# A mixer and mixture-of-experts kernel: weight loads held back behind two row gathers, VectorE work reordered around them, fewer filler products

## The reference, cut to what matters

```python
logits = jnp.dot(t.astype(jnp.float32), router_w.astype(jnp.float32))
probs = jax.nn.softmax(logits, axis=-1)
...
g_idx = jnp.argmax(group_score, axis=-1)            # one of 4 groups of 4 experts
_, loc = lax.top_k(in_group, TOP_K)                 # two experts of the group
combine = ...                                       # weights of the two, in a row of 16
g = jnp.einsum('td,edf->tef', t, w_gate)            # d = 1024, f = 512, e = 16
u = jnp.einsum('td,edf->tef', t, w_up)
a = jax.nn.silu(g) * u * combine[:, :, None]
y = jnp.einsum('tef,efd->td', a, w_down)
return rmsnorm(x + g_f * y, final_norm_g)
```

## Time and profile before

| | |
|---|---|
| median of 3 runs | 761.75 us |
| the runs | 761.73, 763.98, 761.75 us |
| the profiled execution, its own time | 763.88 us |
| its span | 761.5 us |
| TensorE busy | 738.6 us (97%) |
| VectorE busy | 584.9 us (77%) |
| ScalarE busy | 392.0 us (51%) |
| GpSimd busy | 149.2 us (20%) |
| mean granted TensorE clock | 0.995 of full |
| chain of waits, by engine | PE 82%, DVE 9%, DMA 4%, issue 2% |

### The profile page before, as it was taken

The page is one execution under the profiler, slowest core; times in us unless marked ns, Lnnn a source line. Parts: engine busy times, 40 slices in busy tenths (PEclk is TensorE's granted clock), DMA queues, the critical chain, the costliest instruction groups (busy, mean ns, idle before and its releaser), DMA issues.

```text
span 761.5 us, 10492 instructions
## 1 busy us (share of the span) xinstructions
PE 738.6 (97%) x3447; PEld 606.9 (80%) x3447; DVE 584.9 (77%) x709; ACT 392.0 (51%) x360; POOL 149.2 (20%) x121
## 2 busy tenths in 40 slices
PE   7999999999999999999999899999999999999995
PEld 6888888776888888887789677888888888888884
DVE  5884326764675766748768889999999999999985
ACT  5536333424222141323435267777777777777744
POOL 1000004102000000000054272523322323222313
PEclk9999999999999999999999999999999999999999
DMA  8989414211375472927372728799999999999992
GB/s 304 337 290 372 141 56 145 75 57 57 110 248 169 161 250 88 337 72 275 139 246 113 282 73 308 287 398 410 358 358 395 366 375 386 378 396 390 343 182 110
DMA packets 108996, 187.30 MB, mean 246 GB/s; under 512 B 7367, under 2 KB 58631, under 8 KB 108972
## 3 DMA queue, kind: packets, MB, share of 16 engines
q1 hardware_dynamic: 101420, 173.63, 62.9%
q0 software_dynamic: 5936, 11.71, 5.5%
q10 hardware_dynamic: 1616, 1.65, 0.7%
HBM read 180.00 MB, written 15.79 MB: 257 GB/s over the span
## 4 chain that ended last, share of the span: by engine, by line
PE 82%; DVE 9%; DMA 4%; issue 2%; ACT 1%; SPq 1%; POOL 0%; DVEq 0%; POOLq 0%; ACTq 0%
PE ps L1581 25%; PE ps L1583 25%; PE ps L1582 24%; DVE wsplit L893 2%; PE ps L1839 2%; PE ps L1931 1%; PE ps L1711 1%; DMA raw<-in_w_ada 1%; DVE raw L982 1%; DMA raw<-in_w_in 1%; PE ps L1772 1%; DMA raw<-in_w_out 1%; DVE raw L936 1%; PE ps L1875 1%; DMA work<-hf_rows,tok_idx 1%
## 5 line engine op out<-in xcount | busy, mean ns | idle before, releaser
L893 DVE TENSOR_TENSOR wsplit<-raw,wsplit 128x2048 fp32r<-128x2048 f32 x128 | 291.0, 2287 | 67.7 <-ACT wsplit L615 34.6
L802 ACT ACTIVATE wsplit<-raw 128x2048 fp32r<-128x2048 f32 x96 | 183.6, 1919 | 62.4 <-PE ps L1583 62.4
L1581 PE MATMUL ps<-wsplit,hgT 128*128 128x512 f32 x264 | 104.4, 395 | 1.1 <-DVE hgT L1363 1.1
L1583 PE MATMUL ps<-wsplit,hgT 128*128 128x512 f32 x264 | 103.0, 390 | 0.0
L1582 PE MATMUL ps<-wsplit,hgT 128*128 128x512 f32 x264 | 102.8, 389 | 0.0
L1581 PE MATMUL ps<-hT,wsplit 128*128 128x512 f32 x256 | 101.1, 395 | 1.1 <-DVE mx L1078 1.0
L1582 PE MATMUL ps<-hT,wsplit 128*128 128x512 f32 x256 | 99.6, 389 | 0.0
L1583 PE MATMUL ps<-hT,wsplit 128*128 128x512 f32 x256 | 99.6, 389 | 0.0
L936 DVE SCALAR_TENSOR_TENSOR raw<-raw,c_silu 128x256 f32 (+1 forms) x128 | 62.0, 485 | 13.7 <-DMA raw<-in_w_ada 9.7
L1581 PEld LDWEIGHTS ps<-wsplit,hgT 128*128 128x128 f32 x264 | 49.6, 188 | 11.1 <-issue 1.3
L1583 PEld LDWEIGHTS ps<-wsplit,hgT 128*128 128x128 f32 x264 | 49.5, 188 | 10.7
(11 more groups left out here) (310 smaller groups left out, 1214.0 us busy)
## 6 DMA issues: line engine op xcount, KB each, us to landing
raw<-in_w_exp_gate SPq DMA_DIRECT2D x32, 1024.0 KB
raw<-in_w_exp_up SPq DMA_DIRECT2D x32, 1024.0 KB
raw<-in_w_exp_down SPq DMA_DIRECT2D x32, 1024.0 KB
raw<-in_w_in SPq DMA_DIRECT2D x20, 1024.0 KB
raw<-in_w_ada SPq DMA_DIRECT2D x16, 1024.0 KB
raw<-in_w_ada SPq DMA_DIRECT2D x16, 512.0 KB, 5.6
expert_rows<-tmp SPq DMA_DIRECT2D x4, 1024.0 KB, 9.7
raw<-in_w_branch_a SPq DMA_DIRECT2D x4, 1024.0 KB
```

Of the source, the lines that this page charges most:

```text
L802: A_(wsplit[:, c, 0, :], raw[:, c, :], ACT.Copy).then_inc(hi_ready, 1)
L893: V.tensor_tensor(wsplit[:, n, 1, :], raw[:, slot, :], wsplit[:, n, 0, :].bitcast(F32), ALU.subtract).then_inc(lo_ready, 1)
L1581: nc.tensor.matmul(out, w_hi, m_hi_, start=first, stop=False)
L1583: return nc.tensor.matmul(out, w_lo, m_hi_, start=False, stop=last)
```

## The change

Three places change. SP now issues only the first half of `w_down[0]` ahead of a wait for gather 0; the second half follows that, and the two halves of `w_up[1]` wait for gather 1 as well. VectorE does `indices(1)` and tile 0's low rows ahead of the second up chunk's low part and of the two table steps, and `rows_lo(1)` ahead of `select(2, ...)` and of slot 1's low part, where it stood behind both. TensorE issues 7 filler products, not 16, ahead of its wait for gather 0.

```diff
             sp.wait_ge(hf_saved, 16 * NT)
             load(0, w_gate[1, :, 0:4, :], 4)
-            for c in range(2):
-                load(c + 4, w_down[0, :, 2 * c:2 * c + 2, :], 2)
+            load(4, w_down[0, :, 0:2, :], 2)
+            sp.wait_ge(gathered, 16)
+            load(5, w_down[0, :, 2:4, :], 2)
+            sp.wait_ge(gathered, 32)
             for c in range(2):
                 sp.wait_ge(lo_ready, M0 + 3 + c)
                 load(c + 2, w_up[1, :, 4 * c:4 * c + 4, :], 4)
...
             V.tensor_copy(slot_of[:, :], r_slots).then_inc(slots_ready, 1)
             ie = [P, TILES_MAX, E]
-            lo_n(M0 + 3, 3)
-            step(V.tensor_tensor(r_le, iota1[:, 0:TILES_MAX].unsqueeze(2).broadcast_to(ie),
-                                 r_cum.unsqueeze(1).broadcast_to(ie), ALU.is_gt))
-            done()
-            step(V.tensor_reduce(r_n, r_le, AX_X, ALU.add))
-            done()
-
             indices(1)
             for half in range(2):
                 dve.wait_ge((first_hi_half, hg_hi)[half], 1)
...
+            lo_n(M0 + 3, 3)
+            step(V.tensor_tensor(r_le, iota1[:, 0:TILES_MAX].unsqueeze(2).broadcast_to(ie),
+                                 r_cum.unsqueeze(1).broadcast_to(ie), ALU.is_gt))
+            done()
+            step(V.tensor_reduce(r_n, r_le, AX_X, ALU.add))
+            done()
...
             dve.wait_ge(hi_ready, M0 + 5)
             lo(0, 0)
+            rows_lo(1)
             select(2, expert_ahead(0))
...
                 lo_c(1)
                 if not prev:
-                    rows_lo(i + 1)
                     indices(i + 2)
                 lo_c(2)
...
             index(1)
-            unread_products(16)
+            unread_products(7)
             pe.wait_ge(gathered, 16)
```

More of the change, by code:

```diff
@@ L1405, in _ @@
             ie = [P, TILES_MAX, E]
+            indices(1)
+            for half in range(2):
+                dve.wait_ge((first_hi_half, hg_hi)[half], 1)
+                h_half = first_hi[:, 4 * half:4 * half + 4, :].rearrange("p k m -> p (k m)").bitcast(F32)
+                V.tensor_tensor(first_lo[:, 4 * half:4 * half + 4, :].rearrange("p k m -> p (k m)"),
+                                ps[:, 2 + half, :], h_half, ALU.subtract).then_inc((first_lo_half, hg_lo)[half], 1)
             lo_n(M0 + 3, 3)
@@ L1411, in _ @@
             done()
[L1413 to L1418, removed]
             step(V.tensor_tensor(r_le, r_le, r_cum.unsqueeze(1).broadcast_to(ie), ALU.mult))
```

## The result

The changed kernel is slower. Its median is 766.87 us (7 runs, 765.19 to 768.72) against 762.5 us of the kernel before (7 runs beside it, 761.63 to 763.98). The ratio is 1.0056, with a 95% interval of 1.0041 to 1.0071. The forecast was 763.3 us with a range up to 765.7 and no measurable difference; the time lies above the range.

The account below looks back on a forecast made before the run. TensorE, busy for 97% of the span, was taken to bound the kernel, its wait for VectorE at tile 2's gate counting. Gather 0 (0), gather 1 (0) and VectorE's order (+1.5) on 761.75 gave 763.3 us, range 761.2 to 765.7.

Parts of the forecast that it names:

- What bounds the seam: Between 420 and 470 us, the chain runs through POOL's table rows to gather 1, not gather 0, whose gain is swallowed.
- Gather 1 does not follow: POOL's third table-row DMA meets the moved low part, so gather 1 still starts near 440.4: 0 us (-0.3 to +0.9).
- The other moved loads cost nothing: `w_down[0]`'s second half has 20 us until VectorE wants it, and gather 2 is wanted over 10 us on.
- VectorE's order: Behind gather 1, `select(2)` and a low part move behind `rows_lo(1)`; tile 2's gate starts at 472.8, 1.5 us later.
- +1.5: The forecast's sum in us: 0 for gather 0, 0 for gather 1, all of it for VectorE's order.
- The clock rival: Clock falls in the 4.0 us wait for gather 1: +2.4 to +3.3 in all, 764.2 to 765.1 us; chance 0.22.
- The fast rivals: Gather 1 sooner: POOL slips past the low part (762.1 us, 0.12), or free queues shorten its DMAs (759.9 us, 0.08).
- The runs' levels: A median drawn from the runs' upper level, 2.2 us higher (765.5), whatever the change does; chance 0.08.

Follow-up runs that it names:

- first profile: The changed kernel with no further edit, its first profiled execution: 768.72 us, seam 40.36 us from `slot_of` to tile 2's first gate product.
- third profile: The changed kernel run a third time with no further edit: 767.72 us (one run), seam 43.86 us.
- filled variant: The changed kernel with 14 filler products in TensorE's wait for gather 1, ahead of tile 1's turn: median 767.15 us, ratio 1.0056, seam 40.60 us.

## Why the prediction was wrong, point by point

The seam can be split at the start of tile 1's transposes. The last column says what the chain of waits runs through in the second part.

| | `slot_of` to tile 1's transposes | from there to tile 2's gate | bound by |
|---|---|---|---|
| before | 11.96 | 26.28 | TensorE |
| `rows_lo(1)` moved, alone | 11.94 | 27.39 | VectorE's selection, then `index(2)` |
| changed, first profile | 11.86 | 28.50 | second up chunk |
| changed, third profile | 14.97 | 28.89 | TensorE at the lower clock |
| changed, `rows_lo(1)` put back | 15.04 | 28.76 | first up chunk |
| changed, loads put back | 14.91 | 27.86 | TensorE at the lower clock |
| changed, up chunks not held | 14.06 | 28.88 | TensorE at the lower clock |

- **What bounds the seam: right.** Gather 0 was not on the chain, and its 2.7 us were swallowed in the wait for gather 1, which came out at 4.11 us (4.0 forecast). Behind tile 2's gate nothing changed.
- **The step that failed: "Gather 1 does not follow".** Its centre was right for two profiles of three (+ 7.56 by POOL's timeline in both). Its upper bound of + 0.9 was not. I looked for the one POOL DMA that the moved low part would hold up, and let the gather itself start anywhere from 440.1 to 441.4. But `lo(0, 0)` follows some 6 us behind the first low part (5.9 and 6.1 in two profiles), so a gather that is pushed back is caught by the second. My own sum had `lo(0, 0)` end at 443.7 and so start at 441.4, the very bound of the range. And the trace of before showed it as the next catch, which I had not looked at:

```profile
440.64 2.29 DVE L893 TENSOR_TENSOR wsplit<-raw,wsplit 128x2048 fp32r<-128x2048 f32 x1
441.81 2.00 POOL L553 DMA_INDIRECT table_rows<-record,slot_of  x1 [0.30 <-issue]
```

Gather 1, at 440.46, had escaped it by 0.18 us. Measured in the changed kernel's third profile: + 8.73, 2.96 long, landing 3.1 us late, seam + 5.6. The range for this term should have run to +3.1 on the landing and higher on the end.
- **The second term that failed: "The other moved loads cost nothing".** I gave the held-back up chunks 0.4 us, and VectorE's order the rest of the 1.5. Alone, `rows_lo(1)` ahead of `select(2)` does cost 1.1 us of seam, by profile and by time. But in the changed kernel the up chunks bind, and undoing the order saved 0.1 us at most in the one pair of profiles that can be compared. In the first profile ScalarE had the second chunk 8.6 us behind tile 1's transposes (456.59 against 448.03), where I had added 5.0 and 2.9 behind a landing at 444.9. That is the other 0.6 of the 2.12. So the size of +1.5 was near, and its cause was not the one that I gave. The loads have no free place behind gather 0: held back behind gather 1 they bind ScalarE; not held, they delay gather 1 by 2.1 us.
- **The clock rival: its event came, and its price where nothing else bound.** The clock fell in the wait in all three profiles of the changed kernel. In the first, filling the wait kept it up and gave nothing back in the seam. In the third it lies on the chain, though the up chunks bind within 0.4 us of it. With the up chunks not held it costs 2.6 us: 0.9 on the transposes and 1.7 on the products, where the rival had 0.9 and up to 2.8. In the filled variant it fell later, behind tile 2's gate, and cost 1.6 us there.
- **The fast rivals fell.** The third POOL DMA was stretched (1.89 us), and a free queue made none of them shorter than 0.98.
- **The runs' levels: right in size, and not the cause of the miss.** The start differs by up to 4.8 us between executions. I left this 0.08 of a chance. The median of before was 762.5 us over seven runs, where I had built on 761.75 over three; this is 0.75 us of the 3.6 by which the forecast was off. The changed kernel adds a second source of spread, its two seams.

What stays open is the exact share of each seam in the seven runs, since only profiled executions show it. Two seams, at 2.1 and 5.6 over before, frame the median difference of 4.4; whether there are others between them, three profiles do not tell.

## What to carry to other kernels

Before a load or an instruction is moved to make one transfer land sooner, follow the queue of the transfer that the bound waits for; if four small DMAs stand in front of it on another engine, it is those that have to move. Follow as well the semaphores that a moved instruction raises: here a load waited for it, went out 5 to 6 us later, and met the gather that was to be helped. Where two engines exclude each other for microseconds at a time, keep their instructions at a fixed distance from a common event: a start that hangs on a DMA's landing turns a bound of 1 us into a coin toss for 3. Measure such a seam inside single profiles, from one event to another, and take several profiles: one showed 2.1 us of the change's cost, a third 5.6.

## What the runs showed of the hardware

- A POOL DMA instruction that starts while VectorE subtracts one SBUF tile from another ends only some 0.9 us after that subtraction: it took 3.09 us when it started 0.06 us late, and 1.00 when it started 0.05 us early. With three such subtractions back to back it took 6.9 us.
- With weight loads under way a gather of 128 rows took 6.5 to 7.1 us from its issue to TensorE, and 4.1 to 4.5 on quiet queues, where its issue was not caught.
- Behind a wait of 6.27 us the granted clock was 0.50 for 5.8 us of TensorE's work, and cost 2.6 us; behind one of 4.11 us it cost nothing in the seam, since a load bound behind it.
- The granted clock near the start of the program stays low for a time that differs between executions of one kernel, from none to 10 us, and `slot_of` then lies anywhere in 4.8 us.
